# Softmax sums of head pairs inverted together and multiplied into the output, in two attentions of a three-attention kernel

## The chip, the cores and the metric

The kernel runs on one core of a Trainium2 chip. A core has TensorE (matmuls, "PE" in the profile; its weight loads are "PEld"), VectorE (DVE), ScalarE (ACT), GpSimd (POOL) and SyncE (SP), which run side by side and wait for one another by semaphores. Matmuls write to PSUM, eight banks of 128 partitions x 512 fp32; everything else is in SBUF. The metric is the time of one execution on the device in microseconds (us); lower is better.

## The reference

A block of two mixers with a feed-forward part, then two more layers; 512 tokens, width 1024, fp32. Three attentions are in it. The first has 8 heads of 64 and a relative bias, with a convolution branch beside it; the second has 16 heads over 4 key heads, a window of 128, slopes on the distance and a sink; the third is latent attention with 16 heads. What the change touches is the softmax of the first two:

```
z = h @ w_in + b_in                       # q, k, v, glu_a, glu_b, gate_a, gate_b
scores = einsum(q, k) * 64 ** -0.5 + bias
probs = softmax(scores)
a = einsum(probs, v) @ w_attn_o           # first attention; v holds its share of b_in
u = causal_dwconv(glu_a * sigmoid(glu_b)) # 31 taps
u = silu(layer_norm(u)) @ w_conv_o + b_conv_o
y = sigmoid(gate_a) * a + sigmoid(gate_b) * u
...
logits = einsum(q, k) * 64 ** -0.5 - slopes * dist
probs = softmax(concat([logits, sink]))[..., :-1]
y = (einsum(probs, v) * silu(z)) @ w_out  # second attention
```

## The kernel before

Matmuls are kept at fp32 precision by splitting each operand in a high and a low part ("hi", "lo") and adding three products; these are lines L610 to L612 (`mm3`). For weights, ACT rounds the high part (`w_hi`, L1029) and DVE subtracts for the low part (`w_lo`, L1484).

The program for each engine is written out by hand, in loops over steps. An attention is a software pipeline over steps i, where one step is one head and one block of 128 queries; two heads are a pair and take 8 steps. Each engine walks the same steps with its own function `pair_attention`:

- TensorE, step i: scores of the two heads on even steps (L702), the values' matmuls for step i-5 into an output tile (L610 to L612 with `pt_hi`), the transpositions of the probabilities of step i-3 (L732, `turn`), then blocks of other matmuls (`after`): the gates of the first attention (`g` tiles), the gate z of the second (one of 8 blocks per step, so one tile of z in 8 steps).
- ACT, step i: the high part of the transposed probabilities of step i-3 (L1112), the exps of step i (L1083 and L1087, which leave the row sum in `col`), and on odd steps the norm, a multiplication of the probabilities by the inverse of their sum (L1098); then tanh of a gate (L1239) or a weight's high part (L1029), and `ada_product` (L1249) for GpSimd.
- DVE, step i: maxima of the scores (L1587), the reciprocal of a row sum (L1599), the low part of the transposed probabilities (L1615), on even steps the norm (L1609), and every fourth step the eviction of an output tile (`out1` L1728, which adds the bias `b_in`, or `out2` L1906, which multiplies with z). Then its own `after`: a weight's low part (L1484), the convolution's taps (L1561), and at steps 8m the eviction of the z tile (L1922).
- GpSimd adds products up (L520) beside them. It works on SBUF only.

PSUM: banks 4 and 5 hold scores, 6 and 7 transposed probabilities, and the other four take turns as accumulation tiles: tile number n goes to bank n mod 4 (LIN = 4). The numbers are given out ahead by `mixer_tiles` (first attention) and `banded_tiles` (second), in the order in which tiles are finished. `free_bank` makes TensorE wait until tile n-4 has been evicted:

```
if tile >= LIN:
    s, val = ... evicted[tile - LIN]
    pe.wait_ge(s, val)
return ps[:, tile % LIN, :]
```

The convolution's layer norm lies within the first attention: the mean's matmul (L817) waits for the last tap, at step LN_SUM; subtraction follows at step LN_SUB. The third attention already leaves its probabilities unscaled: its sums are inverted per pair (L2025), spread (L2032), turned by four transpositions on TensorE (L990) and multiplied into the output (L2040).

Of the kernel before, what the change touches and what calls it, by code (L numbers as in the profile page):

```python
# [31 lines left out]
P = 128  # L32
# [82 lines left out]
LN_SUM, LN_SUB, LN_SQUARE, LN_SCALE, LN_OUT = 17, 19, 20, 25, 28  # L115
# [10 lines left out]
def mixer_tiles():  # L126

    order = []
    for i in range(NT * H1 + NT + 1):
# [61 lines left out]
def build(nc, t_x, t_w, t_ada, t_vecs, t_ident, t_rope, t_rope_k, t_rel, t_alibi, t_sink, t_p, out, pl_store):  # L191
    with ExitStack() as ctx:
# [26 lines left out]
        col = sb("col", [P, 3, 4])  # L219
# [9 lines left out]
        def at(name, kib, shape, dt=F32):  # L229
# [43 lines left out]
        alibi = at("alibi", 100, [P, 4, 384])  # L273
        zs = at("zs", 92, [P, TOK])
# [39 lines left out]
        v_half, r_ready, p_ready, p_ready_act, t_done, pt_hi_done, pt_ready = sem("v_half"), sem("r_ready"), sem("p_ready"), sem("p_ready_act"), sem("t_done"), sem("pt_hi_done"), sem("pt_ready")  # L314
# [5 lines left out]
            "in_b", "cq", "kr", "kr_sum", "cqn", "ln_sum", "cn", "ch", "cn_sig", "rcol_t", "z_tb", "z_sigb", "z_b", "l_inv", "l_rows", "o3_norm", "v_b", "q_t", "q_r", "q_b", "k_b", "o3_half", "o3", "fin")}  # L320
        R = h_ready
        v_step = sem("v_step")
# [23 lines left out]
        for kind, j in mixer_tiles():  # L346
            tile1[kind, j] = len(evicted)
            evicted.append({"o": (R["o1_half"], j // 2 + 1) if j % 2 == 0 else (tmp_w, tmps_ahead + j // 2 + 1), "g": (R["gate_t"], j + 1), "mean": (R["ln_mean"], CT),
# [14 lines left out]
        o2_at, z_at = {}, {0: LT["a_z"]}  # L363
        for kind, j in banded_tiles():
            (o2_at if kind == "o" else z_at)[j] = len(evicted)
            evicted.append((R["z_t"], j + 1) if kind == "z" else ((R["o2_half"], o_full)[j % 2], j // 2 + 1))
# [14 lines left out]
        class Attn:  # L381
            def __init__(self, heads, n0, q, k, vv, pbuf, pt, spans, lin, over_keys):
                self.heads, self.n0, self.q, self.k, self.v = heads, n0, q, k, vv
                self.p, self.pt, self.spans, self.lin, self.over_keys = pbuf, pt, spans, lin, over_keys
                self.p_at, self.steps = 1 if pbuf is p2 else 0, NT * heads
# [13 lines left out]
        def half(h):  # L399
# [10 lines left out]
                     p1, (pt1_hi, pt1_lo), causal, lambda j: tile1["o", j], [[(0, 0, 2), (1, 1, 2)], [(0, 0, 2), (1, 0, 2), (2, 0, 2), (3, 1, 2)]])  # L410
# [1800 lines left out]
```

## Time and profile before

| | us |
|---|---|
| runs, median of 3 | 1616.21 (1614.96 to 1616.95) |
| profiled execution | 1618.08 |
| its span, first to last instruction | 1616.3 |
| TensorE busy | 1468.8 (91%) |
| DVE busy | 988.3 (61%) |
| ACT busy | 732.9 (45%) |
| GpSimd busy | 236.7 (15%) |

The mean granted clock of TensorE is 0.956 of full speed. The first attention lies between about 198 and 371 us of the span, the second between about 970 and 1113 us. The table of stretches gives the busy time of each engine in a stretch, with the granted clock; the timeline lists instructions of one engine with start and duration, and in brackets the idle time before and what ended it. A row "x4" is a group of four; its duration runs from the first start to the last end.

### The profile page before, as it was taken

What the parts mean: (1) busy time and instruction counts of PE and PEld (TensorE: products, weight loads), DVE (VectorE), ACT (ScalarE), POOL (GpSimd) and SP (SyncE); (2) the same over time, 40 slices, a digit from 0 to 9 for tenths busy, and PEclk for the clock granted to TensorE, in tenths of its full rate; (3) what the DMA queues carried; (4) which work ended last, traced back from release to release, by engine and by line L of the source; (5) the groups of instructions that cost most, each with busy time, mean ns of one, the idle gap of its engine ahead of it and who ended that gap; (6) DMA issues with size and microseconds to landing.
All of it is one profiled execution on the core that took longest, in us unless ns stands there. A gap on an engine that the chain in (4) does not pass through costs nothing.

```text
span 1616.3 us, 19654 instructions
## 1 busy us (share of the span) xinstructions
PE 1468.8 (91%) x6834; PEld 1156.0 (72%) x6834; DVE 988.3 (61%) x1549; ACT 732.9 (45%) x1265; POOL 236.7 (15%) x218
## 2 busy tenths in 40 slices
PE   5898797979987999999998999998999989999897
PEld 3686575767765888887885677776777768778775
DVE  5669878465755555554223647984562568788454
ACT  4424454562324455454123426774442446666442
POOL 3105623231110000000000000111110012222111
PEclk8999799988998999999999999998999999999999
DMA  9532133324621232323322321112222120000221
GB/s 388 192 103 88 56 105 111 110 92 172 219 78 28 102 101 80 104 85 99 102 91 65 98 91 60 59 47 92 80 90 79 55 89 14 27 27 27 105 80 64
DMA packets 39881, 151.65 MB, mean 94 GB/s; under 512 B 4784, under 2 KB 4928, under 8 KB 39040
## 3 DMA queue, kind: packets, MB, share of 16 engines
q1 hardware_dynamic: 29664, 105.92, 20.0%
q0 software_dynamic: 10144, 44.76, 7.6%
q8 instruction: 45, 0.74, 0.2%
q14 instruction: 28, 0.23, 0.0%
HBM read 144.37 MB, written 6.29 MB: 93 GB/s over the span
## 4 chain that ended last, share of the span: by engine, by line
PE 70%; DVE 16%; ACT 7%; issue 5%; DMA 1%; DVEq 0%; POOL 0%; ACTq 0%; SPq 0%; POOLq 0%
PE ps L610 21%; PE ps L611 20%; PE ps L612 20%; DVE w_lo L1484 2%; PE ps L732 2%; PE ps L667 2%; DVE c_acc L1561 2%; ACT w_hi L1029 2%; DVE p L1609 1%; PE ps L702 1%; DMA w_raw<-in_w 1%; PE ps L687 1%; DVE minus_s L1587 1%; DVE pt_lo L1615 1%; DVE tmp L1688 1%
## 5 line engine op out<-in xcount | busy, mean ns | idle before, releaser
L610 PE MATMUL ps<-a_hi,w_hi 128*128 128x512 f32 x880 | 362.3, 412 | 19.7 <-ACTq L1308 11.8
L611 PE MATMUL ps<-a_lo,w_hi 128*128 128x512 f32 x880 | 351.1, 399 | 0.0
L612 PE MATMUL ps<-a_hi,w_lo 128*128 128x512 f32 x880 | 351.0, 399 | 0.0
L1484 DVE TENSOR_TENSOR w_lo<-w_raw,w_hi 128x1024 fp32r<-128x1024 f32 x130 | 166.4, 1282 | 159.6 <-ACT w_hi L1029 158.9
L610 PEld LDWEIGHTS ps<-a_hi,w_hi 128*128 128x128 f32 x880 | 167.9, 191 | 63.6 <-ACTq L1308 12.7
L612 PEld LDWEIGHTS ps<-a_hi,w_lo 128*128 128x128 f32 x880 | 167.6, 190 | 40.2
L611 PEld LDWEIGHTS ps<-a_lo,w_hi 128*128 128x128 f32 x880 | 167.9, 191 | 35.4 <-issue 0.5
L1029 ACT ACTIVATE w_hi<-w_raw 128x1024 fp32r<-128x1024 f32 x138 | 144.4, 1048 | 70.9 <-PE ps L612 55.0
L610 PE MATMUL ps<-b_hi,w_hi 128*128 128x512 f32 x240 | 99.3, 414 | 10.5 <-DVE b_lo L1858 5.6
L611 PE MATMUL ps<-b_lo,w_hi 128*128 128x512 f32 x240 | 96.6, 403 | 0.0
L612 PE MATMUL ps<-b_hi,w_lo 128*128 128x512 f32 x240 | 96.5, 402 | 0.0
L732 PE MATMUL ps<-ident,p 128*128 128x128 f32 x496 | 84.2, 282 | 10.7 <-DVE p L1609 10.4
L1561 DVE SCALAR_TENSOR_TENSOR c_acc<-u_pad,vecs,c_acc 128x512 f32<-128x512 f32 x90 | 85.5, 999 | 0.2
L732 PEld LDWEIGHTS ps<-ident,p 128*128 128x128 f32 x496 | 59.1, 142 | 29.7 <-DVE p L1609 14.0
L1044 ACT ACTIVATE sq<-x_resid 128x512 f32<-128x512 f32 x56 | 35.2, 631 | 98.9 <-DVE x_resid L1937 62.9
L1824 DVE SCALAR_TENSOR_TENSOR c_gate<-u_ff,vecs,c_gate 128x512 f32<-128x512 f32 x44 | 32.9, 748 | 64.4 <-ACT u_ff L1329 64.4
L610 PE MATMUL ps<-g_hi,w_hi 128*128 (+1 forms) x176 | 69.5, 395 | 1.5 <-issue 1.5
L611 PE MATMUL ps<-g_lo,w_hi 128*128 (+1 forms) x176 | 69.4, 394 | 0.0
L612 PE MATMUL ps<-g_hi,w_lo 128*128 (+1 forms) x176 | 69.4, 394 | 0.0
L536 POOL TENSOR_TENSOR sq<-sq 128x512 f32<-128x512 f32 x30 | 38.8, 1293 | 185.9 <-ACT sq L1044 185.9
L1615 DVE TENSOR_TENSOR pt_lo<-ps,pt_hi 128x256 fp32r<-128x256 f32 (+3 forms) x96 | 45.8, 478 | 31.5 <-ACT pt_hi L1112 31.4
L610 PEld LDWEIGHTS ps<-b_hi,w_hi 128*128 128x128 f32 x240 | 46.3, 193 | 24.1 <-issue 6.7
(306 smaller groups left out, 2999.8 us busy)
## 6 DMA issues: line engine op xcount, KB each, us to landing
w_raw<-in_w SPq DMA_DIRECT2D x198, 512.0 KB, 3.5
ada_a<-in_ada POOLq DMA_DIRECT2D x16, 512.0 KB, 7.8
ada_g<-in_ada POOLq DMA_DIRECT2D x16, 512.0 KB, 3.8
ada_b<-in_ada POOLq DMA_DIRECT2D x16, 512.0 KB, 4.3
x_resid<-in_x POOLq DMA_DIRECT2D x2, 2048.0 KB, 11.9
pl_store<-pl_out POOLq DMA_DIRECT2D x2, 2048.0 KB, 8.7
pl<-pl_store POOLq DMA_DIRECT2D x2, 2048.0 KB, 8.7
alibi<-in_alibi POOLq DMA_DIRECT2D x16, 192.0 KB, 2.7
```

The lines of the kernel that those rows point to most:

```text
L536: pool.tensor_tensor(sq[:, 0, :], sq[:, 0, :], sq[:, 1, :], ALU.add).then_inc(sq_used, 1)
L610: pe.matmul(o, w[0], r[0], start=start, stop=False, skip_group_check=skip)
L611: pe.matmul(o, w[0], r[1], start=False, stop=False, skip_group_check=skip)
L612: return pe.matmul(o, w[1], r[0], start=False, stop=stop, skip_group_check=skip)
L667: pe.matmul(ps[:, STAT_BANK, :], ones[:, :], sq[:, q % 2, :], start=(k == 0), stop=(k == n - 1)).then_inc(sq_used, 1)
L732: m = pe.transpose(ps[:, T_BANK + n % 2, P * s:P * s + P], a.p[:, n % 4, a.p_at + P * (s - b):a.p_at + P * (s - b) + P], ident[:, :])
L1029: act.activation(w_hi[:, n % SLOTS, :], w_raw[:, n % RAW, :], ACT.Copy).then_inc(w_hi_done, 1)
L1044: act.activation(sq[:, slot, :], src, ACT.Square).then_inc(sq_ready, 1)
L1484: dve.tensor_tensor(w_lo[:, n % SLOTS, :], w_raw[:, n % RAW, :], w_hi[:, n % SLOTS, :].bitcast(F32), ALU.subtract).then_inc(w_lo_done, 1)
L1561: dve.scalar_tensor_tensor(c_acc[:, f, :], src, w, c_acc[:, f, :], ALU.mult, ALU.add).then_inc(conv_step, 1)
L1615: dve.tensor_tensor(lo_, ps[:, T_BANK + n % 2, turned].rearrange("p (s q) -> p s q", q=P), hi.bitcast(F32), ALU.subtract).then_inc(pt_read ...
L1824: dve.scalar_tensor_tensor(c, u_ff[:, 2 * pair + j, tap:tap + TOK], vecs[:, bass.ds(i * 2 + (VO["w_dwf"] + tap * 2 * FT + w_at + pair), 1) ...
```

## The change

In the first two attentions the probabilities are no longer multiplied by the inverse of their sum; both norms, the reciprocal for each step, and the semaphores between them are gone. The transpositions wait for the exp itself (`e_done`). The sums of both heads of a pair and their four query blocks, eight columns, are collected in `lsum`. Once per pair, DVE takes one reciprocal of the eight (`invert_sums`, step i mod 8 = 0), spreads it to 128x512 (`spread_inverses`, i mod 8 = 1), TensorE turns it by four transpositions into an accumulation tile of its own, kind "l" (`inverses`, i mod 8 = 3), and DVE multiplies the output by it (`divide1`, `divide2`, i mod 8 = 5). `out1` is a plain copy now, and the bias is added behind the division, in the high and low parts of the output. LN_SUB goes from 19 to 18. The third attention uses the same functions, with a wait for the tile instead of for the division two pairs back. Its other steps are as before. There are four pairs in the first and eight in the second attention.

```diff
@@ mixer_tiles and banded_tiles
+        if i % 8 == 3 and i >= 11:
+            order.append(("l", i // 8 - 1))
@@ the second attention's tiles
-            evicted.append((R["z_t"], j + 1) if kind == "z" else ((R["o2_half"], o_full)[j % 2], j // 2 + 1))
+            evicted.append({"z": (R["z_t"], j + 1), "o": (R["o2_half"], j + 1), "l": (o_full, j + 1)}[kind])
@@ TensorE, turn
-                elif n % 2 == 1:
-                    pe.wait_ge(p_ready_act, n // 2 + 1)
                 else:
-                    pe.wait_ge(p_ready, n // 2 + 1)
+                    pe.wait_ge(e_done, n + 1)
@@ TensorE
+            def inverses(a, pair):
+                o = free_bank(a.inv(pair))
+                pe.wait_ge(l_rows, a.pairs_ahead + pair + 1)
+                for t in range(NT):
+                    m = pe.transpose(o[:, P * t:P * t + P], a.spread(pair)[:, P * t:P * t + P], ident[:, :])
+                m.then_inc(lin_done, 1)
...
                     after(i)
+                    if i % 8 == 3 and i >= 11:
+                        inverses(a, i // 8 - 1)
@@ ACT
-                    if 0 <= i - 1 < a.steps:
-                        norms(a, i - 1)
...
-            def outs_of(bufs):
-                return lambda i: hi_of_tmp(bufs[:, i, :])
+            def out1_hi(pair):
+                act.wait_ge(tmp_w, tmps[0] + 1)
+                act.activation(qk_hi[:, pair, :], tmp[:, tmps[0] % 2, :], ACT.Identity, bias=v("b_in", BI_V + pair)).then_inc(hi_done, 1)
@@ DVE, pair_attention
-                    if 0 <= i - 1 < a.steps:
-                        inverse(a.n0 + i - 1)
                     if 0 <= i - 3 < a.steps:
                         pair_turn_lo(a, i - 3)
-                    if 0 <= i - 1 < a.steps:
-                        norms(a, i - 1)
                     if i < a.steps and i % 2 == 0:
                         pair_maxima(a, i + 1)
                     if i % 4 == 1 and i >= 9:
-                        pair_out(i // 4 - 2)
+                        half_out(i // 4 - 2)
+                    if i % 8 == 5 and i >= 13:
+                        divide(i // 8 - 1)
                     after(i)
+                    if i % 8 == 0 and 8 <= i <= a.steps:
+                        invert_sums(a, i // 8 - 1)
+                    if i % 8 == 1 and 9 <= i:
+                        spread_inverses(a, i // 8 - 1)
@@ DVE, the divisions
+            def divide2(pair):
+                inv = bank(attn2.inv(pair))
+                dve.wait_ge(R["o2_half"], 2 * pair + 2)
+                dve.tensor_tensor(o_pair2[:, pair % 2, :], o_pair2[:, pair % 2, :], inv, ALU.mult).then_inc(o_full, 1)
```

TensorE, second attention, step 8 (the first of the six steps 8m at which the gate opens its next tile). `p_107` are the probabilities, `a_hi` and `w_hi` the gate's operands. Before:

```order
L732 MATMUL ps<-ident,p_107 128x128 [waits pt_ready,p_ready_act]
L732 MATMUL ps<-ident,p_107 128x128 x2
L610 MATMUL ps<-a_hi,w_hi 128x512 [waits w_lo_done,o_full]
L611 MATMUL ps<-a_lo,w_hi 128x512
L612 MATMUL ps<-a_hi,w_lo 128x512
L732 MATMUL ps<-ident,p_107 128x128 [waits pt_ready,p_ready]
L732 MATMUL ps<-ident,p_107 128x128
```

Now:

```order
L741 MATMUL ps<-ident,p_107 128x128 [waits pt_ready,e_done]
L741 MATMUL ps<-ident,p_107 128x128 x2
L621 MATMUL ps<-a_hi,w_hi 128x512 [waits w_lo_done,ready_z_t]
L622 MATMUL ps<-a_lo,w_hi 128x512
L623 MATMUL ps<-a_hi,w_lo 128x512
L741 MATMUL ps<-ident,p_107 128x128 [waits pt_ready,e_done]
L741 MATMUL ps<-ident,p_107 128x128
```

The transpositions wait for the exp instead of for the norms; the gate's first matmul waits for `ready_z_t`, the eviction of the tile of z before, instead of `o_full`, an output tile.

DVE, the same step and the start of the next. `z_106` is the gate's tile as evicted, L1587 and L1589 the maxima. Before:

```order
L1599 RECIPROCAL col<-col 128x1 [waits e_done]
L1615 TENSOR_TENSOR pt_lo<-ps,pt_hi 128x3x128 [waits pt_hi_done]
L1585 COPY minus_s<-sink 128x1 [waits e_done,alibi_in3,s_done]
L1587 ISA minus_s,col<-ps,alibi,sink 128x256
L1587 ISA col 128x1
L1922 SCALAR_TENSOR_TENSOR z_106<-ps,rs 128x512 [waits lin_done]
L1599 RECIPROCAL col<-col 128x1 [waits e_done]
L1615 TENSOR_TENSOR pt_lo<-ps,pt_hi 128x2x128 [waits pt_hi_done]
L1609 TENSOR_SCALAR p_107<-p_107,col 128x256 [waits r_ready]
L1906 TENSOR_TENSOR o_pair_113<-ps,z_106 64x256 [waits lin_done,ready_o2,ready_z_a]
```

Now:

```order
L1617 TENSOR_TENSOR pt_lo<-ps,pt_hi 128x3x128 [waits pt_hi_done]
L1587 COPY minus_s<-sink 128x1 [waits e_done,alibi_in3,s_done]
L1589 ISA minus_s,col<-ps,alibi,sink 128x256
L1589 ISA col 128x1
L1940 SCALAR_TENSOR_TENSOR z_106<-ps,rs 128x512 [waits lin_done]
L1602 RECIPROCAL gvec<-gvec 128x8 [waits l_rows,e_done]
L1617 TENSOR_TENSOR pt_lo<-ps,pt_hi 128x2x128 [waits pt_hi_done]
L1918 TENSOR_TENSOR o_pair_114<-ps,z_106 64x256 [waits lin_done,ready_o2,ready_z_a]
L1918 TENSOR_TENSOR o_pair_114<-ps,z_106 64x256
```

The reciprocals and the norm L1609 of before are gone; the eviction of z stands where it did, behind the low part of the transposed probabilities and the second maximum. The eight-column reciprocal and the spreading copy (L1602, L1609) follow.

## Rows read from the trace of the kernel before

**Rows 1.** Table of stretches: length, each engine's busy time, clock, DMA.

```profile
198.00:281.00 83.00, 71.36 (x354) 55.03 (x354) 63.03 (x122) 42.47 (x86) 21.20 (x17) 0.95 0.31 102
281.00:351.00 70.00, 68.28 (x334) 50.09 (x334) 38.98 (x93) 40.33 (x80) 20.18 (x17) 0.96 0.31 105
351.00:371.00 20.00, 10.61 (x47) 9.65 (x47) 10.36 (x16) 9.53 (x17) 6.52 (x6) 0.61 0.36 114
975.00:1085.00 110.00, 106.58 (x717) 82.52 (x715) 95.43 (x311) 79.56 (x214) 14.27 (x18) 1.00 0.19 60
1085.00:1113.00 28.00, 19.41 (x105) 15.67 (x106) 16.06 (x50) 14.84 (x37) 3.09 (x3) 0.76 0.12 36
```

**Rows 2.** TensorE in the timeline, where it waited: start, duration, idle before.

```profile
245.97 0.44 PE L702 MATMUL ps<-qk_hi 64*128 64x384 f32 x2 [2.08 <-DVE col L1587]
...
267.09 0.33 PE L702 MATMUL ps<-qk_hi 64*128 64x128 f32 x2 [1.86 <-DVE col L1587]
...
281.23 3.75 PE L817 MATMUL ps<-c_acc,ones 128*128 128x512 f32 x4 [4.82 <-issue]
...
356.90 1.11 PE L732 MATMUL ps<-ident,p 128*128 128x128 f32 x4 [6.32 <-DVE p L1609]
...
422.76 1.56 PE L687 MATMUL ps<-ones,acc_b 128*128 128x1 f32 x11 [1.99 <-DVE acc_b L1532]
```

**Rows 3.** Groups of instructions, 198 to 366 us: busy, mean, idle.

```profile
L1609 DVE TENSOR_SCALAR p<-p,col 128x128 f32<-128x128 f32 (+3 forms) x16 | 16.2, 1015 | 0.0
...
L1098 ACT ACTIVATE p<-p,col 128x128 f32<-128x128 f32 (+3 forms) x16 | 8.8, 549 | 3.0 <-DVE col L1599 3.0
```

**Rows 4.** DVE in the timeline, first attention.

```profile
229.03 1.41 DVE L1561 SCALAR_TENSOR_TENSOR c_acc<-u_pad,vecs,c_acc 128x512 f32<-128x512 f32 x2
...
258.35 3.76 DVE L1561 SCALAR_TENSOR_TENSOR c_acc<-u_pad,vecs,c_acc 128x512 f32<-128x512 f32 x2
...
353.88 0.15 DVE L1599 RECIPROCAL col<-col 128x1 f32<-128x1 f32 x1
...
354.41 2.44 DVE L1609 TENSOR_SCALAR p<-p,col 128x512 f32<-128x512 f32 x1
```

**Rows 5.** GpSimd in the timeline, the same place as the last row above.

```profile
354.23 2.33 POOL L520 TENSOR_TENSOR acc_p<-acc_p,ada_g 128x1024 f32<-128x1024 f32 x1 [3.02 <-ACT ada_g L1249]
```

**Rows 6.** Groups of instructions of the third attention, 1340 to 1510 us.

```profile
L2040 DVE TENSOR_TENSOR o_pair<-o_pair,ps 128x512 f32<-128x512 f32 x8 | 5.4, 679 | 0.1
...
L2032 DVE COPY sq<-gvec 128x512 f32<-128x512 f32 x8 | 3.3, 418 | 0.0
```

**Rows 7.** TensorE in the timeline, second attention, then third.

```profile
990.22 0.52 PE L732 MATMUL ps<-ident,p 128*128 128x128 f32 x3
990.49 0.48 PE L610 MATMUL ps<-a_hi,w_hi 128*128 128x512 f32 x1
...
1071.11 0.44 PE L702 MATMUL ps<-ka_hi,b_hi 64*128 64x384 f32 x2 [0.31 <-DVE col L1587]
...
1378.35 0.60 PE L990 MATMUL ps<-ident,sq 128*128 128x128 f32 x4
1378.71 0.48 PE L610 MATMUL ps<-k_hi,q_hi 96*128 96x512 f32 x1
```

**Rows 8.** ACT in the timeline at the same step of the second attention.

```profile
990.77 0.49 ACT L1112 ACTIVATE pt_hi<-ps 128x384 fp32r<-128x384 f32 x1 [1.82 <-PE ps L732]
```

**Rows 9.** DVE in the timeline at the same step.

```profile
991.29 0.56 DVE L1615 TENSOR_TENSOR pt_lo<-ps,pt_hi 128x384 fp32r<-128x384 f32 x1 [1.45 <-ACT pt_hi L1112]
...
992.23 0.69 DVE L1922 SCALAR_TENSOR_TENSOR z<-ps,rs 128x512 f32<-128x512 f32 x1
```

**Rows 10.** Table of stretches, behind three of TensorE's gaps; columns as in rows 1.

```profile
246.00:250.00 4.00, 4.00 (x15) 2.98 (x16) 2.61 (x3) 3.05 (x6) 0.86 (x1) 0.57 0.27 83
267.00:271.00 4.00, 3.91 (x26) 3.40 (x27) 2.06 (x5) 4.00 (x8) 0.00 (x0) 1.00 0.01 4
424.00:430.00 6.00, 6.00 (x18) 5.03 (x19) 4.57 (x7) 2.77 (x3) 0.22 (x1) 0.50 0.52 175
```

More of the change, by code:

```diff
@@ L347, in build @@
             tile1[kind, j] = len(evicted)
-            evicted.append({"o": (R["o1_half"], j // 2 + 1) if j % 2 == 0 else (tmp_w, tmps_ahead + j // 2 + 1), "g": (R["gate_t"], j + 1), "mean": (R["ln_mean"], CT),
+            evicted.append({"o": (R["o1_half"], j + 1), "l": (tmp_w, tmps_ahead + j + 1), "g": (R["gate_t"], j + 1), "mean": (R["ln_mean"], CT),
                             "var": (sq_used, SQ["conv"] + CT)}[kind])
@@ L417, in build @@
                      lambda h, s: (vb_hi[:, s, P * (h // 2):P * (h // 2) + P], vb_lo[:, s, P * (h // 2):P * (h // 2) + P]),
-                     p3, (pt3_hi, pt3_lo), full, lambda h: tile3["o", h], [[(s, 0, 2) for s in range(4)], [(s, 2, 4) for s in range(4)]])
+                     p3, (pt3_hi, pt3_lo), full, lambda h: tile3["o", h], [[(s, 0, 2) for s in range(4)], [(s, 2, 4) for s in range(4)]],
+                     lambda pair: tile3["l", pair], lambda pair: sq[:, pair % 2, :])
         used_at = {}
@@ L983, in value_tile @@
                 m.then_inc(lin_done, 1)
-            def inverses(pair):
-                o = free_bank(tile3["l", pair])
-                pe.wait_ge(R["l_rows"], pair + 1)
-                for t in range(NT):
-                    m = pe.transpose(o[:, P * t:P * t + P], sq[:, pair % 2, P * t:P * t + P], ident[:, :])
-                m.then_inc(lin_done, 1)
             def own_head(h):
@@ L1088, in exps @@
                                    accum_out=total).then_inc(e_done, 1)
-            def norms(a, i):
-                n = a.n0 + i
-                if n % 2 == 0:
-                    return
-                b, e = a.spans[a.step(i)[1]]
-                p = a.p[:, n % 4, a.p_at:a.p_at + P * (e - b)]
-                act.wait_ge(r_ready, n + 1)
-                act.activation(p, p, ACT.Copy, scale=col[:, 2, n % 4:n % 4 + 1]).then_inc(p_ready_act, 1)
             def pair_turn_hi(a, i):
@@ L1724, in out1 @@
             def out1(j):
-                src, c = bank(attn1.lin(j)), VO["b_in"] + BI_V + j // 2
+                src, q = bank(attn1.lin(j)), slice(2 * P * (j % 2), 2 * P * (j % 2) + 2 * P)
                 for h in range(2):
-                    m = dve.tensor_scalar(tmp[half(h), tmps[0] % 2, 2 * P * (j % 2):2 * P * (j % 2) + 2 * P],
-                                          src[half(h), 2 * P * h:2 * P * h + 2 * P], vecs[half(h), c:c + 1], None, ALU.add)
-                m.then_inc(tmp_w if j % 2 else R["o1_half"], 1)
-                tmps[0] += j % 2
+                    m = dve.tensor_copy(tmp[half(h), tmps[0] % 2, q], src[half(h), 2 * P * h:2 * P * h + 2 * P])
+                m.then_inc(R["o1_half"], 1)
             def out1_lo(pair):
-                lo_of_tmp(qk_lo[:, pair, :], qk_hi[:, pair, :], R["o1"])
+                his[0] += 1
+                dve.wait_ge(hi_done, his[0])
+                dve.scalar_tensor_tensor(qk_lo[:, pair, :], tmp[:, (tmps[0] - 1) % 2, :], v("b_in", BI_V + pair),
+                                         qk_hi[:, pair, :].bitcast(F32), ALU.add, ALU.subtract).then_inc(R["o1"], 1)
             def mixer_step(i):
@@ L1760, in _, with divide1 @@
             assert tmps[0] == tmps_ahead
-            pair_attention(attn1, out1, mixer_step, out1_lo)
+            def divide1(pair):
+                inv = bank(attn1.inv(pair))
+                dve.wait_ge(R["o1_half"], 2 * pair + 2)
+                slot = tmp_slot()
+                dve.tensor_tensor(slot, slot, inv, ALU.mult).then_inc(tmp_w, 1)
+            pair_attention(attn1, out1, divide1, mixer_step, out1_lo)
             mod_group(2)
```

93 lines of the change are left out of this document (45 added, 48 removed).

## The prediction

> **What bounds the kernel now.** I read the table of stretches first, because busy shares over the whole span mix stages with different limits [rows 1]. In the second attention (975 to 1085 us) TensorE works 106.58 of 110 us at a granted clock of 1.00, while DVE has 95.43 and ACT 79.56 us of work: TensorE sets the time, and all of its idle time there is 3.4 us. In the first attention there are three stretches. From 198 to 281 us TensorE works 71.36 of 83 us: it waits for others. From 281 to 351 us it works 68.28 of 70 us and sets the time. From 351 to 371 us, the tail, it works 10.61 of 20 us at a clock of 0.61. Then I read TensorE's rows with idle time in brackets [rows 2]: before 281 us it waits for the maxima on DVE (gaps of 2.08 and 1.86 us) and 4.82 us ahead of the mean's matmul at L817, which in the program stands behind the last convolution tap (the profile names no releaser); in the tail a transposition waits 6.32 us for the norm on DVE (L1609).
>
> So work that leaves DVE and ACT is worth something before 281 us and in the tail, nothing in between, and in the second attention at most 3.4 us. Any wait that the change gives TensorE in the second attention is paid in full.
>
> **The change part by part.**
>
> *1. First attention up to the mean (198 to 281 us).* A loop runs through both engines per two steps: maxima (DVE), exps and norm (ACT), the gate's tanh and the high half of a weight (ACT), its low half, taps and the other norm (DVE), maxima again. The edit takes a norm out of each engine per two steps: ACT's L1098 is 0.549 us a piece, DVE's L1609 1.015 us [rows 3], and two reciprocals of 0.15 us each [rows 4]. DVE's 1.015 us isn't all to be had. In the tail, a norm of 128x512 lasts 2.44 us [rows 4], and over it GpSimd's addition L520 runs for 2.33 us [rows 5]. Two taps at 229.03 us take 1.41 us together, two at 258.35 us take 3.76 us [rows 4]: whichever DVE operation meets the addition is held up, so without the norm a tap takes the hold-up. I count 0.33 us for the DVE norm, 0.45 for ACT's (starts of neighbours overlap by 0.1) and 0.15 for the reciprocals: 0.93 us per two steps. From about 214 to 281 us, some 6.5 such pairs of steps, this loop and not TensorE sets the pace, so 6.0 us go. Against it, each head pair adds to DVE a 128x512 copy of 0.418 us and a division of 0.679 us (the third attention has both [rows 6]), with a small reciprocal; about 1.1 us lie in this stretch. Sum **-5 us**, ends 0 (the hold-ups fill what is freed) and -9 (DVE's norms count with 1.015 us for six).
>
> *2. From the mean to the end of the gates (281 to 351 us).* TensorE is the bound. It gets two groups of four transpositions; in the third attention, from the start of such a group to the next matmul is 1378.71 - 1378.35 = 0.36 us [rows 7], so 0.7. The new "l" tile takes a place in the rotation of four PSUM banks, so a tile now waits for the fourth tile back in a fuller list; in the first attention this makes the output tile of step 31 wait for the division DVE does two steps earlier, at most about 0.9 us (a third of the 2.3 us of an addition that may hold the division up, on top of almost no slack). Of the 1.7 us of idle time about 0.5 goes. Sum **+1 us**, 0 to +2.
>
> *3. Tail of the first attention.* The transposition at 356.90 us waits for the norm that starts at 354.41. Its exp was there by 353.88 us, when DVE's reciprocal, which waits for it, starts [rows 4]. Without the norm the transposition goes 356.90 - 353.88 = 3.0 us earlier, and I add 1 us since DVE's low half behind it is no longer queued behind the norm either. Late next are the last four transpositions (0.36 us at full clock, about 0.5 here) and the last division, 0.68 us: +1.2. Sum **-3 us**, -5 to -1.
>
> *4. Second attention, new waits.* This is the largest term. Before, each pair of heads takes three PSUM tiles (output, output, gate z), and the gate's first matmul waits for an output evicted long ago. Now it takes four (output, l, output, z), and there are four banks: the tile of z(m+1) needs the bank of z(m). TensorE finishes z(m) in step 8m-1 and opens z(m+1) in step 8m; DVE evicts z(m) in its own step 8m, behind the low half of the turned probabilities (L1615), which waits for ACT's high half (L1112), which waits for TensorE's transpositions right ahead of the gate, and behind a maximum (L1587). All of that is now serial. The profile of before shows each link at m=1: transpositions at 990.22 us, the gate's matmul L610 at 990.49 (nothing to wait for now) [rows 7], ACT's high half at 990.77 [rows 8], DVE's low half at 991.29, and z from 992.23 for 0.69 us to 992.92 [rows 9]. The gate would start at 992.92 instead of 990.49: 2.43 us. TensorE has nothing else in its queue, and behind the waiting matmul stand further transpositions, the gate's next block and the next scores, so everything waits. The order has this wait six times (m = 1 to 6): 6 x 2.43 = **+14.4 us**, with 12 (a hold-up less, 2.0 each) and 17 (2.9 each, where DVE is late, as an eviction held up by an addition would be) as ends.
>
> *5. Second attention, seven groups of transpositions at 0.36 us:* **+2.5 us**.
>
> *6. Gaps there that vanish.* Five of 0.31 us like that at 1071.11 us [rows 7] wait for a maximum; the rest of the 3.4 us is as much DVE's lateness. During each new 2.4 us wait DVE and ACT catch up, so I count all: **-3.4 us**, 0 at worst. That DVE loses 64 reciprocals and 32 norms and ACT 32 norms is otherwise hidden behind TensorE: nothing.
>
> *7. The clock.* After the gap of 2.08 us at 245.97 [rows 2], TensorE ran 4 us with a granted clock of 0.57, so part of it at the lower of its two levels, 1.2 GHz; after the gap of 1.86 us at 267.09 the next 4 us have 1.00; after 1.99 us at 422.76 the next 6 us have 0.50 [rows 2, 10]. So a stall of 2.4 us may bring a fall. One fall costs 4 x 0.43 = 1.7 us up to 6 x 0.50 = 3.0 us. I take four of the six at 1.7: **+6.8 us**, ends 0 and +18 (six of 3.0).
>
> The Trainium skill says in "TensorE: Matmul & The Clock Gate", "A second HAM failure mode: psum-queue depth-cycling", that idling between groups of matmuls while banks are cycled makes the clock oscillate. By that rule all six would fall. The rows above agree for gaps of 2 us and disagree for that of 1.86 us.
>
> *8. Tail of the second attention.* Two norms and reciprocals less, one group of transpositions, one low half later and one division (0.68 us) more: **0**, -2 to +2.
>
> Sum: -5 +1 -3 +14.4 +2.5 -3.4 +6.8 +0 = **+13.3 us**. The profiled execution took 1618.08 us with a span of 1616.3; by it the new one would be 1631.4. The median of the runs is 1616.21, 1.9 lower, so **1629.5 us**.
>
> **Rivals.**
>
> *A, no falls of the clock.* Everything as above without term 7: 1622.7 us. For it: the gap of 1.86 us left the clock alone. Against it: those of 2.08 and 1.99 us [rows 2, 10]. Chance 0.22.
>
> *B, every wait brings a fall.* Six of 3.0 us are 18 instead of 6.8: 1641 us. Chance 0.13.
>
> *C, the other side: the bank is free in time.* If TensorE's queue runs behind DVE at steps 8m, the z eviction has happened when the gate is reached. Then terms 4 and 7 vanish: 1616.2 - 5 + 1 - 3 + 2.5 - 3.4 = 1608.3 us. It decides where DVE's eviction ends before TensorE's transpositions of the same step; but z(m) stands behind the low half of exactly these transpositions in DVE's order, so it can't be earlier unless TensorE itself waits there for something else (in which case DVE's lateness would be a cost of its own). The only way is that the rotation isn't as I read it. Chance 0.06.
>
> *D, the first attention gives more.* If the loop before 281 us gets its whole 1.5 us per two steps and a clock fall with it goes away (-12 instead of -5), and the clock holds in the second attention, the total is 1622.7 - 7 = 1616: no change. Chance 0.08.
>
> *E, the clock stays down among transpositions.* If each stall leaves the clock as the tail of the first attention has it, 0.61 over 20 us [rows 1], and for some 9 us until the next stretch of plain matmuls, each costs 9 x 0.39 = 3.5 us, six 21 us: 1643.8 us. Against it: the second attention has transpositions in each step and runs 110 us at 1.00 [rows 1]. Chance 0.03. The Trainium skill ("TensorE: Matmul & The Clock Gate", "Part 4: PE-mode transpose") says that transposing doesn't count as work for the clock gate; those 110 us speak against it for this mixture.
>
> **How the numbers follow.** The forecast itself has 0.48. The range from **1614 to 1642 us** takes in A, B and D with the ends of terms 1, 4 and 7, and leaves out C, E and the far ends. This kernel's runs can tell 0.2% (3.2 us) from no change. Faster by more: C and a part of D, 0.08; within: most of D and the low end of A, 0.10; slower: **0.82**.
>
> **What would show it.** In the profile after, the gate's first matmul (L621) of six steps has an idle time of 2 to 3 us before it, put down to DVE's z (L1940), and nothing like it elsewhere in that attention; its stretch is 12 to 22 us longer; DVE's busy time in it falls without a gain; some rows of it show a clock below 1.00. The mean's matmul comes some 5 us earlier, the gap of 6.32 us shrinks below 4. The prediction is wrong if L621 has no such waits, if the six waits are well under 2 us because DVE, relieved of norms, gets to z sooner, or if the first attention moves by more than 10 us.

## The result, and the profile after

| | before | after |
|---|---|---|
| median of 5 runs, us | 1616.95 (1614.96 to 1618.52) | 1627.37 (1624.15 to 1629.82) |
| profiled execution, us | 1618.08 | 1629.82 |
| its span, us | 1616.3 | 1628.0 |

The changed kernel takes 1.0063 of the time before, with a 95% interval of 1.0047 to 1.008: 10.4 us slower, where 13.3 had been forecast. The profiled execution is the slowest of the five. The first attention got shorter, and the second lost more than twice as much.

The table of stretches of the changed kernel, cut at the same places of the program as [rows 1], to about a us: length, busy time of PE, PEld, DVE, ACT and POOL, granted clock, share of DMA and GB/s.

```profile
199.00:277.00 78.00, 72.50 (x359) 56.84 (x359) 60.11 (x103) 39.30 (x78) 21.14 (x18) 0.93 0.33 108
277.00:347.00 70.00, 67.20 (x339) 50.06 (x339) 37.30 (x77) 38.10 (x73) 20.27 (x17) 0.98 0.32 105
347.00:363.00 16.00, 8.21 (x54) 7.52 (x53) 11.38 (x16) 8.54 (x15) 6.31 (x5) 0.79 0.37 120
968.00:1098.00 130.00, 115.05 (x740) 89.55 (x738) 86.31 (x246) 69.33 (x190) 14.21 (x18) 0.95 0.16 51
1098.00:1120.00 22.00, 13.89 (x103) 11.48 (x104) 14.56 (x42) 11.71 (x29) 2.56 (x3) 0.94 0.00 0
```

The stretch before the mean has gone from 83 to 78 us, the tail of the first attention from 20 to 16. The main part of the second attention took 110 us for 717 matmul records and takes 130 for 740, with 15 us of idle time on TensorE where 3.4 us were, and the clock is at 0.95 of full speed instead of 1.00. DVE (95.43 to 86.31 us) and ACT (79.56 to 69.33) have less to do there, and the stretch is longer all the same.

TensorE in the timeline of the changed kernel, the second attention (start, duration, idle time before and its releaser):

```profile
984.92 0.79 PE L621 MATMUL ps<-a_hi,w_hi 128*128 128x512 f32 x1 [2.24 <-DVE z L1940]
...
1004.34 0.50 PE L621 MATMUL ps<-a_hi,w_hi 128*128 128x512 f32 x1 [2.24 <-DVE z L1940]
...
1023.96 0.50 PE L621 MATMUL ps<-a_hi,w_hi 128*128 128x512 f32 x1 [2.24 <-DVE z L1940]
...
1043.50 0.50 PE L621 MATMUL ps<-a_hi,w_hi 128*128 128x512 f32 x1 [2.23 <-DVE z L1940]
...
1061.59 0.50 PE L621 MATMUL ps<-a_hi,w_hi 128*128 128x512 f32 x1 [2.23 <-DVE z L1940]
...
1081.12 0.50 PE L621 MATMUL ps<-a_hi,w_hi 128*128 128x512 f32 x1 [2.23 <-DVE z L1940]
```

These are the six waits, all at the gate's first matmul, all put down to DVE's eviction of z. Between the first scores of the second attention (968.21 us) and 1098 us, only one other idle time above 0.2 us is in the trace (0.64 us, at 975.43). The first of the six, link by link; TensorE, then ACT, then DVE:

```profile
982.17 0.51 PE L741 MATMUL ps<-ident,p 128*128 128x128 f32 x3
```

```profile
982.72 0.49 ACT L1112 ACTIVATE pt_hi<-ps 128x384 fp32r<-128x384 f32 x1 [1.82 <-PE ps L741]
```

```profile
983.24 0.56 DVE L1617 TENSOR_TENSOR pt_lo<-ps,pt_hi 128x384 fp32r<-128x384 f32 x1 [1.51 <-ACT pt_hi L1112]
...
983.78 0.47 DVE L1589 CUSTOM_DVE_ANT_0 minus_s<-ps,alibi,sink 128x256 f32<-128x256 f32 x1
...
984.17 0.69 DVE L1940 SCALAR_TENSOR_TENSOR z<-ps,rs 128x512 f32<-128x512 f32 x1
```

The chain is that of [rows 7 to 9], started 8 us earlier: transpositions, high half, low half, second maximum, z, and 0.06 us after z has ended (984.86) the gate begins.

TensorE's granted clock in 4 us behind four of the six stalls:

```profile
984.00:988.00 4.00, 3.08 (x8) 2.14 (x8) 1.53 (x6) 0.97 (x4) 0.00 (x0) 0.57 0.00 0
1004.00:1008.00 4.00, 3.66 (x14) 2.60 (x14) 1.94 (x6) 1.82 (x4) 0.00 (x0) 0.61 0.01 2
...
1044.00:1048.00 4.00, 4.00 (x27) 3.07 (x27) 2.79 (x8) 2.71 (x7) 0.00 (x0) 1.00 0.00 0
...
1082.00:1086.00 4.00, 4.00 (x29) 3.21 (x28) 3.17 (x10) 3.08 (x8) 0.00 (x0) 1.00 0.00 0
```

It fell behind four of the six (0.57, 0.61, and behind the third and the fifth 0.57 and 0.58) and stayed at 1.00 behind two, though all six stalls are 2.23 or 2.24 us long.

### The profile page after: what moved, and what is told of

Same layout as the page of the kernel before. It is cut to its first block, busy times and chain, and to the rows that moved or that the text cites. A ratio compares the mean times of both kernels' runs of the same rounds, so it can differ in the third digit from the quotient of the medians.

```text
span 1628.0 us, 19690 instructions
## 1 busy us (share of the span) xinstructions
PE 1474.2 (91%) x6882; PEld 1163.0 (71%) x6882; DVE 975.3 (60%) x1441; ACT 713.7 (44%) x1217; POOL 236.9 (15%) x218
## 4 chain that ended last, share of the span: by engine, by line
PE 73%; DVE 14%; ACT 6%; issue 5%; DMA 1%; DVEq 0%; POOL 0%; ACTq 0%; SPq 0%; POOLq 0%
PE ps L621 22%; PE ps L622 21%; PE ps L623 21%; PE ps L741 3%; DVE w_lo L1485 2%; ACT w_hi L1040 2%; DVE c_acc L1562 2%; PE ps L713 2%; PE ps L678 1%; DMA w_raw<-in_w 1%; PE ps L698 1%; DVE tmp L1692 1%; DVE a_lo L1697 1%; DVE x_resid L1813 0%; DVE acc_b L1533 0%
## 5 line engine op out<-in xcount | busy, mean ns | idle before, releaser
L1562 DVE SCALAR_TENSOR_TENSOR c_acc<-u_pad,vecs,c_acc 128x512 f32<-128x512 f32 x90 | 91.9, 1070 | 0.2
L1112 ACT ACTIVATE pt_hi<-ps 128x256 fp32r<-128x256 f32 (+3 forms) x96 | 41.4, 432 | 90.2 <-PE ps L741 89.8
L741 PEld LDWEIGHTS ps<-ident,p 128*128 128x128 f32 x496 | 60.5, 144 | 23.6 <-issue 9.9
```

The lines of the kernel that those rows point to most:

```text
L741: m = pe.transpose(ps[:, T_BANK + n % 2, P * s:P * s + P], a.p[:, n % 4, a.p_at + P * (s - b):a.p_at + P * (s - b) + P], ident[:, :])
L1112: act.activation(hi, ps[:, T_BANK + n % 2, turned].rearrange("p (s q) -> p s q", q=P), ACT.Copy).then_inc(pt_hi_done, 1)
L1562: dve.scalar_tensor_tensor(c_acc[:, f, :], src, w, c_acc[:, f, :], ALU.mult, ALU.add).then_inc(conv_step, 1)
```

## Experiments

The kernels of one comparison ran on the same chip as the kernel before; each ratio is to it.

### One step of DVE moved: z evicted first

```diff
 def pair_attention(a, half_out, divide, after, pair_lo=None, early=None):   # DVE
     for i in range(a.steps + 2 * NT):
+        if early is not None:
+            early(i)                 # evict_z: at i = 8f the two lines below
         if i < a.steps and i % 2 == 0:
             pair_maxima(a, i)
...
-                if k == 0 and f < KT:
-                    dve.wait_ge(lin_done, z_at[f] + 1)
-                    dve.scalar_tensor_tensor(z2[:, f, :], ps[:, z_at[f] % LIN, :], 0.5, r, ALU.mult, ALU.mult).then_inc(R["z_t"], 1)
```

> The changed kernel with one step of DVE moved: in the second attention the gate's tile z is evicted first in step 8m, ahead of both maxima and of the low half of the turned probabilities. Theory (the bank of z holds TensorE up): the six idle times of 2.24 us before the gate's matmul go, with the four clock falls behind them (1.7 us each): 1627.4 - 13.4 - 6.8 = 1607 us, within 3. Rival (the wait only takes the place of lateness of DVE, which TensorE would meet one step later, at the scores): the idle time moves to the scores' matmul, and the time stays above 1620.

Measured: 1605.11 us (1604.43 to 1606.5), 0.9933 of before, interval 0.9909 to 0.9958. That is faster than both kernels. DVE, then TensorE, in the same step:

```profile
977.08 0.56 DVE L1617 TENSOR_TENSOR pt_lo<-ps,pt_hi 128x384 fp32r<-128x384 f32 x1 [1.08 <-ACT pt_hi L1112]
977.56 0.68 DVE L1941 SCALAR_TENSOR_TENSOR z<-ps,rs 128x512 f32<-128x512 f32 x1
```

```profile
978.80 0.52 PE L741 MATMUL ps<-ident,p 128*128 128x128 f32 x3
979.08 0.48 PE L621 MATMUL ps<-a_hi,w_hi 128*128 128x512 f32 x1
```

z is gone from its bank by 978.24 us, and the gate opens at 979.08 right behind the transpositions, with no idle time. The stretch, with columns as above:

```profile
965.00:1082.00 117.00, 113.35 (x785) 90.23 (x785) 91.44 (x267) 74.03 (x204) 14.33 (x18) 1.00 0.18 56
```

Its clock is 1.00 throughout. From the first scores of the second attention to its last, the changed kernel takes 138.5 us and z_first 117.6, a difference of 20.9 us; before, it took 118.7. So the new waits, with what they did to the clock, are the whole loss. From one opening of the gate to the next, without a fall of the clock, the changed kernel takes 18.09 us (1043.50 to 1061.59), z_first 15.66 (979.08 to 1057.36 in five): a stall shown as 2.24 us costs 2.43. With a fall in it the period is 19.54 us (1023.96 to 1043.50): a fall costs 1.45 (the four periods with a fall are 19.42 to 19.62 us).

### The rotation alone, without the change

The kernel before, with one more tile per pair that nobody reads:

```diff
 def banded_tiles():
...
+        if i % 8 == 3 and i >= 11:
+            order.append(("skip", i // 8 - 1))
...
+            if kind == "skip":
+                skipped[j] = len(evicted)
+                evicted.append(evicted[-LIN])
+                continue
...
                     after(i)                                   # TensorE
+                    if a is attn2 and i % 8 == 3 and i >= 11:
+                        o = free_bank(skipped[i // 8 - 1])
+                        pe.transpose(o[:, 0:P], ident[:, :], ident[:, :]).then_inc(lin_done, 1)
```

> The kernel before, norms and reciprocals kept, with nothing of the change but one more accumulation tile per pair in the second attention: a single 128x128 transposition of the identity at the place of the four, which nobody reads. Theory (the fuller rotation alone makes the waits): six idle times of 2.2 to 3 us before the gate's matmul L616, put down to z, and 1631 to 1640 us. Rival (it takes the inverses, divisions and the changed order on DVE to hold TensorE up): 1617 to 1620 us, no such idle times.

Measured: 1638.72 us (1637.36 to 1640.72), ratio 1.0137, interval 1.0113 to 1.0162.

```profile
993.96 0.50 PE L616 MATMUL ps<-a_hi,w_hi 128*128 128x512 f32 x1 [2.24 <-DVE z L1931]
...
1032.12 0.59 PE L616 MATMUL ps<-a_hi,w_hi 128*128 128x512 f32 x1 [3.09 <-DVE z L1931]
```

Norms, reciprocals and everything else as before, and yet the six waits are there. So the fuller rotation makes them by itself. Five of them are longer than in the changed kernel (2.24, 2.57, 3.09, 2.71, 2.70, 2.69 us). Ahead of the third, the norm of the step before takes 1.90 us, beside an operation of GpSimd (L567, 1.28 us from 1028.58), and puts DVE behind; ahead of the stall of 2.24 us the same norm takes 0.34 us (989.96).

```profile
1028.12 1.90 DVE L1618 TENSOR_SCALAR p<-p,col 128x256 f32<-128x256 f32 x1
```

What the change saves on DVE in the second attention thus shows here, as shorter stalls.

### Shorter and longer stalls

z evicted between the low half and the second maximum (z_mid), and z evicted twice in its old place (z_twice):

```diff
         if 0 <= i - 3 < a.steps:                # z_mid
             pair_turn_lo(a, i - 3)
+        if early is not None:
+            early(i)
```

```diff
     dve.wait_ge(lin_done, z_at[f] + 1)          # z_twice
+    dve.scalar_tensor_tensor(z2[:, f, :], ps[:, z_at[f] % LIN, :], 0.5, r, ALU.mult, ALU.mult).then_inc(z_pre, 1)
+    dve.wait_ge(z_pre, f + 1)
     dve.scalar_tensor_tensor(z2[:, f, :], ps[:, z_at[f] % LIN, :], 0.5, r, ALU.mult, ALU.mult).then_inc(R["z_t"], 1)
```

> The changed kernel with z evicted between the low half of the turned probabilities and the second maximum. Theory: each of the six waits is shorter by the maximum, about 0.45 us: 1.8 instead of 2.24 us, -2.7 us in all. For the clock two theories: if a stall has to be about 2 us long to bring a fall (as the rows of before with 1.86 and 2.08 us), the four falls go too: 1618 us; if falls come whatever the size in this range, some four stay: 1624.5 us.

> The changed kernel with the eviction of z done twice (the same values). Theory: each of the six waits is longer by one eviction, 0.6 us: 2.85 us, +3.6 us. If every stall of that length brings a clock fall (six instead of four at 1.7 us) 1634.5 us, if their number stays 1631 us. Rival (DVE's work is hidden): 1627.5 us, no change.

Measured: z_mid 1622.99 us (ratio 1.0036, interval 1.0023 to 1.0048), z_twice 1635.25 us (1.0114, 1.0088 to 1.0141). One stall of each; the window behind a stall of z_mid is below them:

```profile
1034.40 0.50 PE L621 MATMUL ps<-a_hi,w_hi 128*128 128x512 f32 x1 [1.77 <-DVE z L1941]
```

```profile
986.21 0.50 PE L621 MATMUL ps<-a_hi,w_hi 128*128 128x512 f32 x1 [2.96 <-DVE z L1942]
```

```profile
1035.00:1039.00 4.00, 4.00 (x17) 2.62 (x16) 2.14 (x5) 1.92 (x5) 0.00 (x0) 0.57 0.00 0
```

| kernel | each stall, us | falls behind the six | time, us |
|---|---|---|---|
| z_first | none | 0 | 1605.1 |
| z_mid | 1.77 | 1 | 1623.0 |
| changed kernel | 2.24 | 4 | 1627.4 |
| z_twice | 2.96 | 5 | 1635.3 |
| extra_tile | 2.24 to 3.09 | 4 | 1638.7 |

The times are medians; the changed kernel's is from another comparison. The falls are counted in one profiled execution of each, and vary: with stalls of 2.23 or 2.24 us like the changed kernel's, three other traces (dve_norm_kept, act_norm_kept and after_short_adds, below) have 3, 3 and 2 of six. Neither clock theory held as stated: z_mid has one fall behind a stall of 1.77 us, and the five other stalls of that size have none, so the size does not decide alone. Its median, 1623.0 us, lies nearer the figure for falls that stay (1624.5) than the one for falls that go (1618). The stalls themselves were forecast well: 1.8 and 2.85 us, and 1.77 and 2.96 came.

That longer stalls bring more falls is not shown: extra_tile has longer ones than the changed kernel and as many falls. At the short end there is one more row of evidence. In the third attention of the changed kernel TensorE waits six times 1.53 us for DVE (the first at 1370.56 us), and from 1350 to 1490 us the clock is 1.00 throughout; the kernel before has six such waits too (1.52 us), without a fall.

### The first attention alone

The change is kept in the first attention; in the second the norms, reciprocals and three tiles per pair are back:

```diff
# TensorE, turn
                     pe.wait_ge(s_free, n - n2 + 1)
+                elif a is attn2:
+                    pe.wait_ge(p_ready_act if n % 2 else p_ready, i // 2 + 1)
                 else:
                     pe.wait_ge(e_done, n + 1)
...
-                    if i % 8 == 3 and i >= 11:
+                    if a is attn1 and i % 8 == 3 and i >= 11:
                         inverses(a, i // 8 - 1)
# DVE (ACT likewise with its norms)
+                    if a is attn2 and 0 <= i - 1 < a.steps:
+                        inverse(a.n0 + i - 1)
                     if 0 <= i - 3 < a.steps:
                         pair_turn_lo(a, i - 3)
+                    if a is attn2 and 0 <= i - 1 < a.steps:
+                        norms(a, i - 1)
```

> The change in the first attention alone; the second keeps norms, reciprocals and three tiles per pair. Theory: the first attention ends 7 us earlier as in the changed kernel, the rest is as before: 1618.0 - 7 = 1611 us, and z_first (1605.1) stays some 2 us or more below it by the second attention's tail. Rival (the earlier end of the first attention is given back at the transition): 1616 to 1618 us.

Measured: 1610.65 us (1608.54 to 1612.14), ratio 0.9953, interval 0.9935 to 0.9971. So the first attention's part is worth 6.8 us by these runs, and 7 was expected. The second's part turns from a loss of some 17 us into a gain of a few with z first (1605.11 against 1610.65, in different comparisons; by the ratios the gain is 3 us).

### What the norms of the first attention were worth

One norm put back at a time, as a multiplication by 1.0 in the old place:

```diff
# dve_norm_kept; act_norm_kept is the same on ACT, for odd n, as a Copy with scale 1.0
+                if a is not attn1 or n % 2 != 0:
+                    return
+                dve.wait_ge(e_done, n + 1)
+                dve.tensor_scalar(p, p, 1.0, None, ALU.mult).then_inc(p_ready, 1)
...
+                elif a is attn1 and n % 2 == 0:        # TensorE, turn
+                    pe.wait_ge(p_ready, n // 2 + 1)
```

> The changed kernel with one part undone in the first attention: DVE still multiplies the probabilities of even steps, in the old place, by 1.0, without reciprocals, and the transpositions of those steps wait for it. The distance from the first scores to the mean is 77.9 us in the changed kernel, 82.9 in the kernel before. Theory of the prediction (a DVE norm is worth its short form, 0.33 us per two steps, since a tap takes the hold-up): 77.9 + 2.1 = 80.0 us. Rival (the norm's full 1.0 us counts): 82 us or more. Rival (ACT's norm was the whole price): 78.0 us. In the tail of the first attention the transposition behind the last even step's norm waits 2 to 3 us longer.

> The same for ACT: on odd steps ACT multiplies the probabilities by 1.0 in the old place. Theory (0.45 us per two steps on the loop): from the first scores to the mean 77.9 + 2.9 = 80.8 us. Rival (ACT's norm lies beside the limit, since ACT waits for DVE's maxima anyway): 78.0 us, no change.

TensorE's first scores and the mean's matmul, in the changed kernel, in dve_norm_kept and in act_norm_kept:

```profile
199.12 0.47 PE L713 MATMUL ps<-qk_hi 64*128 64x128 f32 x2 [11.22 <-issue]
...
276.98 5.37 PE L836 MATMUL ps<-c_acc,ones 128*128 128x512 f32 x8 [2.58 <-issue]
```

```profile
197.38 0.47 PE L713 MATMUL ps<-qk_hi 64*128 64x128 f32 x2 [10.92 <-issue]
...
279.04 3.36 PE L838 MATMUL ps<-c_acc,ones 128*128 128x512 f32 x4 [4.28 <-issue]
```

```profile
197.83 0.48 PE L713 MATMUL ps<-qk_hi 64*128 64x128 f32 x2 [11.21 <-issue]
...
278.05 4.60 PE L838 MATMUL ps<-c_acc,ones 128*128 128x512 f32 x5 [4.88 <-issue]
```

The distances are 77.86, 81.66 and 80.22 us. By them DVE's norm is worth 3.8 us, nearly twice the 2.1 I gave it and just below the rival's 82 us; ACT's is worth 2.4 of the 2.9. Each is from one trace, and the distance isn't quite fixed: z_first, z_mid and attn1_only, with the same first attention as the changed kernel, have 78.0, 77.9 and 77.9 us, but z_twice has 78.8, and its first scores come early (197.44 us), as in the two traces here. Against z_twice the norms are worth 2.9 and 1.4 us.

One expectation failed: in the tail, the transposition behind the last even step's norm waits 2.54 us in dve_norm_kept, where a low half makes it wait 2.30 in the changed kernel, and not 2 to 3 us longer; the tail as a whole is 1.2 us longer. The whole times are 1634.95 and 1634.54 us in two runs each, 7 us above the changed kernel and more than these distances explain. In act_norm_kept the stretch from the mean to the last scores is longer as well (65.5 us for 62.1, at a clock of 0.93 for 0.97). And the stretch between the two attentions, which no experiment alters, takes 606.4 us in z_first's trace, 609.8 in the changed kernel's and 611.4 in dve_norm_kept's (clocks of 0.98, 0.97 and 0.97), so whole times of single traces can differ by 5 us for nothing that an edit did.

The groups of the convolution's taps, all 33 of them ahead of the mean, in the kernel before and in the changed one (busy time, mean of one in ns):

```profile
L1561 DVE SCALAR_TENSOR_TENSOR c_acc<-u_pad,vecs,c_acc 128x512 f32<-128x512 f32 x33 | 28.1, 878 | 0.2
```

```profile
L1562 DVE SCALAR_TENSOR_TENSOR c_acc<-u_pad,vecs,c_acc 128x512 f32<-128x512 f32 x33 | 34.2, 1067 | 0.2
```

The same 33 taps take 6.1 us more. Of the 16 norms [rows 3] eight lie ahead of the mean; in the kernel before they take 9.6 us:

```profile
L1609 DVE TENSOR_SCALAR p<-p,col 128x128 f32<-128x128 f32 (+3 forms) x8 | 9.6, 1202 | 0.0
```

So DVE got 3.5 us free there and not 9.6, or 0.44 per norm. In dve_norm_kept, norms and taps are:

```profile
L1607 DVE TENSOR_SCALAR p<-p 128x128 f32<-128x128 f32 (+3 forms) x8 | 9.9, 1243 | 0.0
...
L1564 DVE SCALAR_TENSOR_TENSOR c_acc<-u_pad,vecs,c_acc 128x512 f32<-128x512 f32 x33 | 28.1, 878 | 0.2
```

With the norms back, the taps are at 28.1 us again, and both together are 3.8 us more than the 34.2 us, as the distance says. The prediction had this mechanism: the hold-up by GpSimd's addition goes to a tap. It left 0.33 us per norm.

### Without the hold-ups

```diff
# GpSimd, in both kernels
-                    pool.tensor_tensor(acc[:, :], acc[:, :], ada_g[u % 2][:, :], ALU.add)...
+                    pool.tensor_tensor(acc[:, 0:8], acc[:, 0:8], ada_g[u % 2][:, 0:8], ALU.add)...
```

> The kernel before with GpSimd's additions L520 cut from 1024 to 8 columns (so the modulation of the later norms is computed wrongly), to take away what holds DVE up in the first attention. Theory (term 1: each addition holds up whatever DVE operation it meets by about 1.5 to 2.3 us): no DVE norm or pair of taps above 1.6 us before the mean, the DVE loop is shorter, and the mean comes 4 us or more earlier than 281.23 - 198.35 = 82.9 us after the first scores. Rival (the hold-ups lie beside the limit): 82 us or more.

> The changed kernel with the same cut. Theory (the norms removed are worth only their short form, since a tap takes the hold-up): the distance of both kernels from the first scores to the mean, 82.9 - 77.9 = 5.0 us with the additions, stays between 2 and 6 us without them. Rival (the change gains by taking operations away that could be held up): under 1.5 us.

Both kernels leave 1016 of the 1024 columns of these sums out. Measured, one run each: 1600.41 us and 1612.52 us. The first scores and the mean's matmul, kernel before and then changed kernel, both with short additions:

```profile
197.28 0.47 PE L702 MATMUL ps<-qk_hi 64*128 64x128 f32 x2 [11.14 <-issue]
...
269.17 2.05 PE L817 MATMUL ps<-c_acc,ones 128*128 128x512 f32 x2 [3.02 <-issue]
```

```profile
197.46 0.48 PE L713 MATMUL ps<-qk_hi 64*128 64x128 f32 x2 [11.38 <-issue]
...
268.86 2.38 PE L836 MATMUL ps<-c_acc,ones 128*128 128x512 f32 x5 [1.00 <-issue]
```

The distances are 71.9 and 71.4 us. So the additions cost the kernel before 11 us up to the mean, where 4 or more were expected, and the two kernels differ by 0.5 us where they had differed by 5.0: the rival's figure. The taps and the eight norms of the kernel before, then the taps of the changed kernel:

```profile
L1561 DVE SCALAR_TENSOR_TENSOR c_acc<-u_pad,vecs,c_acc 128x512 f32<-128x512 f32 x33 | 23.7, 747 | 0.2
```

```profile
L1609 DVE TENSOR_SCALAR p<-p,col 128x128 f32<-128x128 f32 (+3 forms) x8 | 3.0, 379 | 0.0
```

```profile
L1562 DVE SCALAR_TENSOR_TENSOR c_acc<-u_pad,vecs,c_acc 128x512 f32<-128x512 f32 x33 | 23.6, 746 | 0.2
```

This gives the accounts of the hold-ups. Before, they were 6.6 us on norms (9.6 less 3.0) and 4.4 on taps (28.1 less 23.7), together the 11 us of the distance. In the changed kernel they are 10.6 us on taps (34.2 less 23.6): 6.1 of the 6.6 us have passed on.

Up to the mean, the change gains only as long as the additions slow DVE. The rival gives as the reason that the norms caught the hold-ups; but nearly all of these passed on. What the traces show is that TensorE sets the pace once the additions are short. In the kernel before with short additions it is busy without a gap from 210 to 266 us:

```profile
210.00:266.00 56.00, 56.00 (x301) 44.08 (x299) 43.24 (x102) 34.70 (x70) 8.38 (x17) 1.00 0.44 141
```

The changed kernel with short additions has 56.00 of 56.00 us there too, so less work for DVE shortens nothing. The theory's range of 2 to 6 us overlooked this.

### The bank of the inverses in the first attention

The trace of the changed kernel has new waits there too:

```profile
261.22 0.55 PE L621 MATMUL ps<-pt_hi,v_hi 128*128 128x256 f32 x1 [2.79 <-DVE tmp L1771]
...
300.69 1.12 PE L843 MATMUL ps<-sq,ones 128*128 128x512 f32 x2 [1.39 <-DVE tmp L1771]
...
330.58 0.50 PE L621 MATMUL ps<-a_hi,w_hi 128*128 128x512 f32 x1 [0.89 <-ACT gate_b L1240]
```

The values' matmul at 261.22 and the convolution's at 300.69 us wait for a division (L1771), which frees the bank of the inverses. For the third the profile names ACT's eviction of a gate, ahead of which ACT loads an activation table (1.28 us). One experiment moved the tile, on top of z_first:

```diff
-        if i % 8 == 3 and i >= 11:
+        if i in (12, 20, 28, 35):            # mixer_tiles, and the same on TensorE
             order.append(("l", i // 8 - 1))
```

> z_first with one step moved in the first attention: for its first three pairs TensorE turns the inverses one step later (steps 12, 20, 28), so that the output tile of the next pair waits for an output's eviction and not for the division behind it. Theory (the idle time of 2.79 us before the values' matmul at 261.22 us is a wait for the bank that the division frees): it shrinks by one division and a bit, 0.7 to 1.5 us, 1604 us; 1601 to 1602 us if the clock fall behind it (6.83 us at half) goes as well. Rival (that matmul really waits for DVE being late, whatever the bank): 1605 us, the gap stays at 2.5 us or more.

Measured: 1606.84 us (1603.62 to 1609.9), ratio 0.9927, interval 0.9903 to 0.9952; no difference from z_first that these runs can show (two near 1604 and two near 1610; the profile is of one of the slower).

```profile
260.09 0.36 PE L621 MATMUL ps<-pt_hi,v_hi 128*128 128x256 f32 x1 [2.04 <-DVE tmp L1734]
...
276.65 2.04 PE L836 MATMUL ps<-c_acc,ones 128*128 128x512 f32 x2 [5.09 <-issue]
```

The gap is 0.8 us shorter, 2.04 instead of 2.83 in z_first (2.79 in the changed kernel), and its releaser is now the eviction of an output (L1734), so the bank was what it waited for. The clock doesn't fall behind it any more: 1.00 from 260 to 264 us, where z_first has 0.59. But a new wait of 1.07 us for DVE's maxima follows at 263.79, and the wait for the mean grew from the 4.05 us of z_first to 5.09. Its distance from the first scores (79.1 us, from 197.56 us) is no shorter than z_twice's 78.8: before the mean DVE sets the pace, and what TensorE saves there it waits for later.

## Why the prediction was right, step by step

| term | forecast, us | measured, us | from |
|---|---|---|---|
| 1, up to the mean | -5 | -5.0 | first scores to mean, 82.9 and 77.9 |
| 2, to the last scores | +1 | +1.2 | 60.8 and 62.1 |
| 3, tail | -3 | -4.1 | last scores to last values, 23.4 and 19.4 |
| 4, six waits | +14.4 | +14.6 | 6 x 2.43, changed kernel against z_first |
| 5 and 6, transpositions less gaps | -0.9 | -1.2 | first to last scores, 118.7 before, 117.6 in z_first |
| 7, clock | +6.8 | +5.8 | four falls at 1.45 |
| 8, tail of the second attention | 0 | -1.3 | last scores to next stage, 14.1 and 12.9 |

Differences are taken before rounding. The spans differ by 11.7 us (1616.3 and 1628.0). The terms sum to 10.0; the remaining 1.7 are 0.8 us that the first attention starts later, 0.6 more at the end of the second's scores, and what lies outside both. Spans are those of the profiled executions, and the changed kernel's is its slowest of five, 2.4 us above its median.

Term 4 held in every link (its own product, 6 x 2.43, is 14.6 and not 14.4). It could be read from three facts: the tile list says whose eviction the gate waits for, the order says what stands ahead of that eviction on DVE, and one step of the trace of before [rows 7 to 9] has the duration of each link. The rival with the bank free in time (1608 us) is the right picture of another kernel: z_first, at 1605.

Term 1 came out at its total and with the right mechanism, and with sizes that were off: that -5 came out so exactly is partly luck. DVE's norm was put at 0.33 us per two steps and is 0.44 to 0.58 (2.9 to 3.8 over 6.5), ACT's at 0.45 and is 0.22 to 0.36. That the hold-ups pass to the taps held for 6.1 of 6.6 us.

Term 2 had one new wait of 0.9 us and put it at step 31, on a division. The trace has 1.39 us for a division at 300.69 and 0.89 for ACT; so the new waits are 2.3 us and not 0.9, and the places are others. That the term is right all the same is partly luck: in the same stretch the clock rose from 0.96 [rows 1] to 0.98. The wait of 2.79 us at 261.22, for the first pair's division, is in no term: two held-up taps (3.75 us, from 255.43) had put DVE behind. It cost little because the mean waits for DVE anyway.

Term 3: the gap of 6.32 us became two of 2.3 and 2.2. For the first, DVE gets to the low half only at 349.22, when a weight's low half and two products of the convolution are done (from 346.87 us); for the second, the low half stands behind a held-up operation, the bias with the low half of an output (L1738, 2.86 us). How much of the 4.1 us is the norm's is open, since the norm put back costs the tail 1.2 us:

```profile
349.91 1.09 PE L741 MATMUL ps<-ident,p 128*128 128x128 f32 x4 [2.30 <-DVE pt_lo L1617]
353.16 1.09 PE L741 MATMUL ps<-ident,p 128*128 128x128 f32 x4 [2.16 <-DVE pt_lo L1617]
```

```profile
349.22 0.55 DVE L1617 TENSOR_TENSOR pt_lo<-ps,pt_hi 128x384 fp32r<-128x384 f32 x1
349.68 2.86 DVE L1738 SCALAR_TENSOR_TENSOR qk_lo<-tmp,vecs,qk_hi 128x512 fp32r<-128x512 f32 x1
352.47 0.54 DVE L1617 TENSOR_TENSOR pt_lo<-ps,pt_hi 128x384 fp32r<-128x384 f32 x1
```

Term 7 was the least certain, and four of six was a choice and not a result: that the trace has four is luck, since three others with the same stalls have 3, 3 and 2. A fall costs 1.45 us and not 1.7 to 3.0; the end of 3.0 us came from the row at 422.76 [rows 2], where eleven matmuls of one column each follow the gap, and nothing like them follows the six stalls. The Trainium skill ("TensorE: Matmul & The Clock Gate", "A second HAM failure mode: psum-queue depth-cycling") tells of a kernel in which idling between groups of matmuls, while banks are cycled, made the clock oscillate. That is what happened here. It doesn't say how often; read as in the prediction, every stall, it would have given all six.

The step LN_SUB 19 to 18 and the bias behind the division were not tried apart.

## What to carry to other kernels

Where PSUM banks rotate by a fixed list, one more tile per period changes whose eviction every tile waits for: write out the new list, and look for a tile that now waits for one finished a step before. If there is such a tile, put its eviction first in the evicting engine's step, ahead of whatever waits for TensorE's own next work; here that one move was worth 21 us in the second attention (138.5 to 117.6), with medians of 1627.4 and 1605.1. And work taken off an engine whose operations take longer beside another engine's counts less than its rows say: take the difference of busy time over the whole stretch, neighbours included.

## What was not expected of the hardware

GpSimd's additions of 128x1024 (some 2.4 us each, 14 in the first attention, six of them before the mean) cost the kernel before about 11 us up to the mean; with 8 columns, the distance from the first scores to the mean falls from 82.9 to 71.9 us. A 128x512 tap takes 747 ns without them and 878 ns (before) or 1067 ns (changed kernel) on the mean with them.

Equal stalls of 2.24 us don't always bring the lower clock: 4, 3, 3 and 2 of six in four traces. Stalls of 1.77 us did it once in six, those of 1.53 us in the third attention never. A stall's cost is also some 0.2 us above its idle time (2.43 for 2.24 us; 1.96 for 1.77 in z_mid and 3.18 for 2.96 in z_twice, whose gates open 17.62 and 18.84 us apart without a fall).
